# Three of eight experts with 96 token slots in place of 128: float32 products on 64-, 32- and 32-column tiles of TensorE

## The reference

```
logits = h @ router                        # 256 tokens x 8 experts
top_val, top_idx = top_k(logits, 2); gates = softmax(top_val)
out = sum over e of (silu(h @ w_gate[e]) * (h @ w_up[e])) @ w_out[e] * combine[:, e]
```

## Time and profile before

| | us |
|---|---|
| median of 3 runs | 2230.64 |
| the profiled execution's own time | 2228.06 |
| its span, first to last instruction | 2226.3 |
| first gate product of stage 0 to the end of the span | 1247.5 to 2226.3 |
| stages 0, 2, 4, 6 (WIDE) | 143.8, 153.0, 153.0, 153.0 |
| stages 1, 3, 5, 7 (HALF) | 87.4, 87.4, 87.4, 89.5 |

### The profile page before, as it was taken

The page is one execution under the profiler, slowest core; times in us unless marked ns, Lnnn a source line. Parts: engine busy times, 40 slices in busy tenths (PEclk is TensorE's granted clock), DMA queues, the critical chain, the costliest instruction groups (busy, mean ns, idle before and its releaser), DMA issues. The chain is left out here.

```text
span 2226.3 us, 26662 instructions
## 1 busy us (share of the span) xinstructions
PE 2032.2 (91%) x11494; PEld 1420.3 (64%) x11494; DVE 609.5 (27%) x1266; ACT 314.5 (14%) x600; POOL 41.1 (2%) x65
## 2 busy tenths in 40 slices
PE   5998897888999989789887799999999999999997
PEld 3876886786888867688776444554455445544454
DVE  4436565553000046355663100000000000000002
ACT  1012222210000033222220100000000000000001
POOL 0001000000000000000000000000000000000000
PEclk9999998999999999888987899999999999999998
DMA  8729321102344152000000797999799978998794
GB/s 337 297 83 425 135 116 76 77 4 81 147 155 152 39 236 76 6 10 10 10 1 5 301 398 283 408 427 376 285 359 427 427 284 311 426 428 332 271 418 199
DMA packets 37081, 492.11 MB, mean 221 GB/s; under 512 B 4380, under 2 KB 4541, under 8 KB 7325
## 3 DMA queue, kind: packets, MB, share of 16 engines
q1 hardware_dynamic: 36956, 490.33, 54.7%
HBM read 487.95 MB, written 2.36 MB: 220 GB/s over the span
## 5 line engine op out<-in xcount | busy, mean ns | idle before, releaser
L1935 PE MATMUL bank<-ring,arena 128*128 128x512 f32 x896 | 395.7, 595 | 1.7 <-DMA ring<-in_experts 1.7
L1935 PEld LDWEIGHTS bank<-ring,arena 128*128 128x128 f32 x896 | 167.5, 190 | 208.8 <-issue 208.8
L1938 PE MATMUL bank<-ring,arena 128*64 128x256 f32 x1792 | 204.7, 381 | 0.0
L1970 PE MATMUL bank<-ring,arena 128*128 128x512 f32 x448 | 197.2, 593 | 0.0
L2132 DVE TENSOR_TENSOR arena<-bank,arena 128x512 f32<-128x512 f32 (+1 forms) x56 | 31.3, 558 | 597.4 <-PE bank L1935 314.1
L1938 PEld LDWEIGHTS bank<-ring,arena 128*64 128x64 f32 x1792 | 125.5, 137 | 81.1 <-issue 23.8
L1229 PE MATMUL bank<-arena,ring 128*128 128x256 f32 x704 | 155.3, 382 | 4.0 <-DVE arena L290 3.8
L1970 PEld LDWEIGHTS bank<-ring,arena 128*128 128x128 f32 x448 | 84.8, 190 | 106.8 <-issue 106.8
L1229 PEld LDWEIGHTS bank<-arena,ring 128*128 128x128 f32 x704 | 134.0, 191 | 24.5 <-issue 4.1
L2088 ACT ACTIVATE arena<-bank 128x512 f32<-128x512 f32 (+1 forms) x56 | 27.6, 492 | 787.2 <-PE bank L1935 493.5
L1350 PE MATMUL bank<-arena,ring 128*128 128x256 f32 x512 | 115.6, 388 | 6.4 <-DVE arena L290 3.8
(11 more groups left out here) (357 smaller groups left out, 2002.2 us busy)
## 6 DMA issues: line engine op xcount, KB each, us to landing
ring<-in_experts SPq DMA_DIRECT2D x168, 2048.0 KB, 13.3
ring<-in_stream SPq DMA_DIRECT2D x61, 2048.0 KB, 11.5
arena<-in_masks SPq DMA_DIRECT2D x1, 1280.0 KB, 5.9
xT<-in_xT SPq DMA_DIRECT2D x1, 1024.0 KB, 6.2
arena<-in_s0gd SPq DMA_DIRECT2D x4, 256.0 KB, 2.8
out_sgd<-arena SPq DMA_DIRECT2D x4, 256.0 KB, 2.5
out_y<-arena SPq DMA_DIRECT2D x4, 256.0 KB, 2.5
arena<-in_hfw SPq DMA_DIRECT2D x1, 544.0 KB
```

Of the source, the lines that this page charges most:

```text
L1935: mm = nc.tensor.matmul(out[:], h[:, j, :], w[:, j, :], start=start, stop=stop)
L1938: mm = nc.tensor.matmul(out[HALF * x:HALF * x + HALF, 0:256], h[:, j, 0:HALF], w[:, j, 256 * x:256 * x + 256], start=start, stop=stop, til ...
L1970: mm = nc.tensor.matmul(ps[6 + h][:], aT[:, f, :], w[:, f, 512 * h:512 * h + 512], start=start, stop=stop)
```

## The change

The stages of ranks 1, 2 and 3 (q = 2, 4, 6) get 96 slots. The MID code of `in_product` and `project` is rewritten: a block is five products, one of 64 stationary columns x 384 streamed at column 0, one of 32 x 384 at column 64, and three of 32 x 128 at column 96. What each partition holds at the end is the same as with the twelve products. The 64-column product needs its tokens side by side in `actT`, so `copied` writes MID's activations in two instructions in place of one. `result` needs no edit: for MID it makes two copies of 96 x 384 and six of 32 x 128.

```diff
-        MAIN_CAPS = [WIDE, HALF] * 4
+        MAIN_CAPS = [WIDE, HALF] + [MID, HALF] * 3
...
                     else:
+                        for lo, hi in ((0, HALF), (HALF, MID)):
+                            nc.tensor.matmul(out[lo:hi, 0:3 * P], h[:, j, lo:hi], w[:, j, 0:3 * P], start=start, stop=stop,
+                                             tile_position=(0, lo), skip_group_check=True)
                         for r in range(3):
-                            for x in range(4):
-                                u, o = (x, r * P) if x < 3 else (r, 3 * P)
-                                mm = nc.tensor.matmul(out[32 * x:32 * x + 32, r * P:(r + 1) * P], h[:, j, 32 * u:32 * u + 32],
-                                                      w[:, j, o:o + P], start=(start and r == 0), stop=stop,
-                                                      tile_position=(0, 32 * x), skip_group_check=True)
+                            mm = nc.tensor.matmul(out[MID:P, r * P:(r + 1) * P], h[:, j, 32 * r:32 * r + 32], w[:, j, 3 * P:4 * P],
+                                                  start=(start and r == 0), stop=stop, tile_position=(0, MID), skip_group_check=True)
...
                         else:
+                            o = 512 * h
+                            for lo, hi in ((0, HALF), (HALF, MID)):
+                                nc.tensor.matmul(ps[6 + h][lo:hi, 0:3 * P], aT[:, f, lo:hi], w[:, f, o:o + 3 * P], start=start, stop=stop,
+                                                 tile_position=(0, lo), skip_group_check=True)
                             for r in range(3):
...
+                                mm = nc.tensor.matmul(ps[6 + h][MID:P, r * P:(r + 1) * P], aT[:, f, 32 * r:32 * r + 32],
+                                                      w[:, f, o + 3 * P:o + 4 * P],
+                                                      start=(start and r == 0), stop=stop, tile_position=(0, MID),
+                                                      skip_group_check=True)
...
-                n = m.width(i)
-                nc.scalar.activation(actT[:, i % 2].rearrange("p f t -> p (f t)")[:, 0:n], ps[4][:, 0:n], ACT.Copy).then_inc(m.aT, 1)
+                n, aT = m.width(i), actT[:, i % 2]
+                if m.caps[i // KC] == MID:
+                    blocks = ps[4][:, 0:n].rearrange("p (r t) -> p r t", r=3)
+                    nc.scalar.activation(aT[:, 0:3, 0:MID], blocks[:, :, 0:MID], ACT.Copy)
+                    nc.scalar.activation(aT[:, 3, 0:MID].rearrange("p (r t) -> p r t", r=3), blocks[:, :, MID:P], ACT.Copy)\
+                        .then_inc(m.aT, 1)
+                else:
+                    nc.scalar.activation(aT.rearrange("p f t -> p (f t)")[:, 0:n], ps[4][:, 0:n], ACT.Copy).then_inc(m.aT, 1)
```

## The result

The changed kernel takes 2583.45 us (median of 3 runs, 2580.82 to 2588.32) where the kernel before takes 2230.64: slower, by a ratio of 1.1585 (95% interval 1.1556 to 1.1615). The prediction was 2592.

A forecast was written before the change was run, and what follows sets the result against it. TensorE was taken to bound the kernel, with DMA not far behind. 2228.1 us plus 365 for the blocks, less 4 for the rest, gave 2589 profiled; the median lies 2.6 above, 2592. Range 2125 to 2630.

The forecast's parts named there:

- The bound: TensorE bounds the expert stages; in the changed MID stages no TensorE wait on the ring, DMA share below 0.6.
- The block: A MID block runs 64-column and 32-column products in turn, with two width changes: 1.58 us against WIDE's 0.859.
- The price of the change: Each change between 64- and 32-column tiles: 0.09 us with nothing streaming, 0.05 on the first matmul, 0.14 us together.
- the small terms: MID transposes -4.6 us, gather -2.6, width changes after transposes +2.9, together -4; ScalarE's two activation copies hidden.
- The sum: Over three MID stages, 504 blocks at +0.725 us give +365, the rest -4: 2589 us profiled, 2592 as median.
- the bounds given with it: For the MID blocks: no loss at width changes but no overlap, +224 us; 0.03 us more a block, +380.
- Rival one: In MID blocks the three tiles run side by side, 0.66 us a block: 2129 to 2149 us; chance 0.34.
- Rival two: MID tiles run side by side, but instruction supply over a busy DMA takes back the gain: 2228 us; chance 0.06.

The follow-up runs named there:

- split kernel: Changed kernel with its 64 x 384 product made as two of 32 x 384, so all tiles have one width: 2139.36 us, 0.9594 of the kernel before.
- regrouped kernels: Changed kernel's products reordered in each weight tile, 64-column ones two or eight at a time before the 32-column ones: 2514.60 and 2460.26 us.

## Why the prediction was right, point by point

- **The bound.** TensorE, whole stages long, before and after; no wait on the ring in the MID stages, and no part for ScalarE or VectorE. As stated, down to the DMA share of 0.52 there (below 0.6 was forecast).
- **The block.** Forecast 1.58 us, measured 1.57. The step on which the sum hung, that 64- and 32-column tiles aren't in flight together although their columns are disjoint, was a guess from changes between overlapping tiles. The rows of the kernel before couldn't decide it, and the prediction gave it 0.59 against 0.34. The split kernel settles it: with equal widths on the same columns the block is 0.65 us. The rule of the Trainium skill, TensorEngine Tiling (Array Packing), section Key Properties, that a change of tiling mode drains TensorE, holds for disjoint tiles as well: the 0.60 us of idle weight loads before 1600.39 show it in the changed kernel.
- **The price of the change.** 0.14 us from three changes in the earlier trace rows; the regrouped kernels give 0.137 and 0.144. The forecast was too high by 0.014 us a block, 7 us in all: the six short matmuls take 6 x 0.109 = 0.654 us where 0.66 was reckoned, and two changes take 1.57 - 0.644 - 0.654 = 0.27 us where 0.28 was. The change into 32-column tiles is the cheaper one; its first matmul is some 0.02 us longer and not 0.05.
- **The sum.** 504 x (1.57 - 0.859) = 358 us, where 365 was forecast. The stages grew by 352.7 us together, which leaves -5.6 for the small terms, where -4 was forecast; they weren't measured one by one. 2592 lies 8.5 us above 2583.45, and it would have been 2.7 more but for the later start of stage 0, which the sum doesn't have: that much of the closeness is luck. The upper end of the range, 2630, doesn't follow from the bounds given with it: +380 gives 2607. The result doesn't touch either.
- **The small terms.** ScalarE's copies, forecast at 410 and 256 ns, take 412 and 246, and TensorE waits for neither. Hidden.
- **Rival one** was wrong for this kernel and right for its neighbour: 2129 to 2149 us was its time, and the kernel of one width takes 2139. Its pair of 206.5 us, TensorE's and DMA's pace at once, is what the first pair took (206.5, at 423 to 424 GB/s); the second took 208.8. The tens of microseconds of waits on the ring came to some 10 in all, since TensorE is hardly faster than DMA there.
- **Rival two** named the supply of instructions at 14 matmuls a microsecond as a danger, and discounted it by a burst of 33 a microsecond for 2.28 us. At 18 a microsecond within a block, the pace of six products, it does nothing. At 37, the pace of twelve, it costs 158 us against the split kernel. A burst of 76 matmuls is shorter than the 128 that one packet of instructions brings, so that row could not have shown it.

## What to carry to other kernels

Side by side on TensorE's columns means one tile width for all, as far as 64 and 32 columns show it: before packing products of unequal token counts, cut them all to the narrowest width, even at the price of more products. If widths must mix, group them, since each change costs 0.14 us and no overlap crosses it. And merge what can be merged within the width (here 12 products into 6), because many short matmuls beside a full DMA run out of instructions (2297 us with twelve, 2137 with six).

## What the runs showed of the hardware that was not expected

- A long stretch of 32 x 128 matmuls at 37 a microsecond stops, mostly after 128 matmuls or two or three times as many, for up to 3.2 us while weight transfers move 306 GB/s, and far more rarely when they move 89. Instructions come in packets of 16.4 KB, about 256 instructions each, and the matmuls go on 1.2 to 1.6 us behind one. The MID stages of the split kernel, at 18 a microsecond within a block, have no such stop with DMA at 423 GB/s.
- The order of the program isn't kept between tiles of one width. In the code both matmuls of the 32 x 384 product stand ahead of the third tile's six. In the trace of the changed kernel its second one starts at 1487.00, behind three of those six, which start from 1486.66 on: it is as if each column tile went through its own work. Across a change of width no such overtaking stands in the traces shown here.
